# A hybrid encoder step: input projection, gated linear attention and convolution merged into one program on one core

## The chip, the cores and the metric

One Trainium2 chip, one core of it. The metric is the device time of one execution in microseconds (us). The engines are called TensorE (PE in the rows; its weight loads PEld), VectorE (DVE), ScalarE (ACT), GpSimd (POOL) and SyncE (SP, which only issues DMAs here). Each runs its own instructions in order and waits on semaphores.

## The reference

One layer over 2048 tokens of a new stream and 64 tokens of a running one, width 1024, all in float32:

```python
x = layer_norm(x, ln_in_g, ln_in_b)
gq, gk, gv, gr, glow, sq, sk, sv, cb, cc, ch = split_cols(x @ w_in)   # 3088 columns
lg = log_sigmoid(glow @ w_gate_up + b_gate) / 16
# gated linear attention, 4 heads, blocks of 64 tokens with a state S
b = cumsum(lg); att = einsum('bhtk,bhsk,bhtsk->bhts', q, k, exp(b_t - b_s))   # causal
o = (q * exp(b)) @ S + att @ v
S = exp(b_last) * S + (k * exp(b_last - b))^T @ v
go = o * rsqrt(mean(o*o) + eps) * gla_norm_g * silu(gr)
# stick-breaking attention so over sq, sk, sv;  convolution
co = cb * causal_conv3(cc * ch)
mix = concat(go, so, co) @ w_out
x = LN(alpha * x + mix);  x = LN(alpha * x + relu(x @ w_up)^2 @ w_down)
```

The outputs are both x, the new keys and values sk and sv, the attention states and the last two rows of cc * ch of each stream.

## The kernel before

Three programs follow each other, with a barrier of all engines between them: `phase_in`, `phase_gla`, `phase_tail`. They hand data on through scratch memory in HBM (`zt_scratch`, features by tokens; `gv_scratch`, tokens by features; `mixt_scratch`; `xn_scratch`).

**phase_in** normalises x in tiles of 128 tokens (ScalarE's square root, three VectorE instructions, one addition on POOL), stores the normalised rows, transposes them on TensorE (`ps_t`, L357) and splits them into a high and a low part (`xh`, `xl`, double-buffered by token group). The token groups are 512, 512, 512 and 576 tokens long. Weights come in six chunks of 512 or 528 columns, each loaded again for each token group, copied by ScalarE (L272, `wh`) and reduced by VectorE to a low part (L329, `wl`). A product is three float32r matmuls for each of eight slices of the contraction (`split_product`, L111 to L113): xh by wh, xh by wl, xl by wh. "F" units have features in rows and up to 512 tokens as columns; "T" units (gv, keys and values) have 128 tokens in rows and 512 features as columns. Six PSUM banks hold results, ScalarE evacuates them (L279) and issues their stores.

**phase_gla** works in groups of 512 tokens (and the 64 of the running stream), and within a group in tiles of 128 tokens. Work "ahead" for a group: the gate (TensorE, ScalarE), the running sum of it (`gate_sum`, VectorE scans), `decay`, and six levels: for each, VectorE forms differences of sums (`level_arg`, L744, L745), ScalarE takes exp (L661), VectorE multiplies with k and q (`level_mul`, L754, L760), TensorE forms products (`level_product`, L859) and VectorE writes the valid part into `att` (`level_put`, L790); the diagonal follows (L866). Work for a tile, here called a body: k's transpose (`turn`), `kv` (L891), `intra` (L903), `inter` (L924), the new state (L809), the squares' sums (L934), root, and gating (L820, L823). The list `order` interleaves a group's bodies with the next group's ahead. POOL works through the convolution on its own: ten pieces of 512 (or 64) tokens, for each three loads, a product and six instructions, a store, all issued on POOL's queue (L948 to L983).

**phase_tail** does the stick-breaking attention, the output projection and the feed-forward block. It has its own loads of constants (L1360) and is not touched.

The lines that follow are the functions that the diff touches.

Of the kernel before, what the change touches and what calls it, by code (L numbers as in the profile page):

```python
# [114 lines left out]


# [3 lines left out]
def phase_in(nc, x_tile, ln_g, ln_b, w_in, ident_in, xn_dram, zt_dram, token_stores, lasting):  # L120
    WW = 528
    chunks = [
        ([(C_GQ, 512)], "F", Z_GQ),
        ([(C_GR, 528)], "F", Z_GR),
        ([(C_GV, 512)], "T", "gv"),
        ([(C_SQ, 256), (C_CB, 256)], "F", Z_SQ),
        ([(C_SK, 512)], "T", "kv"),
        ([(C_CC, 512)], "F", Z_CC),
    ]
    NCH = len(chunks)  # L130
    WSTAGE, OUTS, BANKS = 4, 4, 6
    s = Scope(nc, "p1")
    with s:
        ident = s.sb("ident", [P, P])
        g_b = s.sb("g_b", [P, D])
        b_b = s.sb("b_b", [P, D])
        xs = s.sb("xs", [P, 2, D])
        xn = s.sb("xn", [P, 2, D])
        stats = s.sb("stats", [P, 2, 12])
        mv = s.sb("mv", [P, 2, 2])  # L140
        rstd = s.sb("rstd", [P, 2, 1])
        eps = s.sb("eps", [P, 1])
        xh = s.sb("xh", [P, 2, KT, NMAX], F32R)
        xl = s.sb("xl", [P, 2, KT, NMAX], F32R)
        wst = s.sb("wst", [P, WSTAGE, WW])
        wh = s.sb("wh", [P, 2, KT, WW], F32R)
        wl = s.sb("wl", [P, 2, KT, WW], F32R)
        outb = s.sb("outb", [P, OUTS, 512])
        ps_t = s.ps("ps_t", [P, 2, 512])
        ps_m = s.ps("ps_m", [P, BANKS, 512])  # L150

        ident_loaded, rows_in = s.sem("ident_loaded"), s.sem("rows_in")
        eps_set = s.sem("eps_set")
        x_in = s.sems("x_in", 2)
        stats_done = s.sem("stats_done")
        var_done = s.sem("var_done")
        std_done = s.sem("std_done")
        rstd_done = s.sem("rstd_done")
        centred = s.sem("centred")
        scaled = s.sem("scaled")  # L160
        normed = s.sem("normed")
        xn_out = s.sems("xn_out", 2)
        turned = s.sem("turned")
        xhi_done = s.sem("xhi_done")
        xlo_done = s.sem("xlo_done")
        w_inn = s.sems("w_in", WSTAGE)
        whi_done = s.sem("whi_done")
        wlo_done = s.sem("wlo_done")
        unit_done = s.sem("unit_done")
        evacuated = s.sem("evacuated")  # L170
        out_st = lasting.results


        gtiles, n = [], 0
        for (t0, cnt) in GROUPS:
            gtiles.append([(n + i, o, c) for i, (o, c) in enumerate(subtiles(t0, cnt, P))])
            n += len(gtiles[-1])

        units = []
        for g, (t0, cnt) in enumerate(GROUPS):  # L180
            for c, (pieces, kind, where) in enumerate(chunks):
                gc = g * NCH + c
                width = sum(w for _, w in pieces)
                if kind == "F":
                    for m0 in range(0, width, P):
                        mw = min(P, width - m0)
                        for o, cc in moving(cnt):
                            units.append(dict(g=g, gc=gc, kind="F", m0=m0, mw=mw, o=o, n=cc, t0=t0, row=where + m0))
                else:
                    for o, cc in subtiles(t0, cnt, P):  # L190
                        units.append(dict(g=g, gc=gc, kind="T", o=o, n=cc, t0=t0, what=where))
        by_chunk = {}
        for i, u in enumerate(units):
            by_chunk.setdefault(u["gc"], []).append((i, u))
        chunk_end = {gc: us[-1][0] + 1 for gc, us in by_chunk.items()}

        order = [("norm", 0, gtiles[0][0]), ("weights", 0)]
        for i, t in enumerate(gtiles[0]):
            order += [("norm", 0, x) for x in gtiles[0][i + 1:i + 2]] + [("turn", 0, t)]
        for g in range(len(GROUPS)):  # L200
            for c in range(NCH):
                gc = g * NCH + c
                if gc + 1 < NCH * len(GROUPS):
                    order.append(("weights", gc + 1))
                ahead = [(g + 1, t) for t in gtiles[g + 1][c:c + 1]] if g + 1 < len(GROUPS) else []
                order += [("norm", *x) for x in ahead] + [("product", gc)] + [("turn", *x) for x in ahead]

        block = s.stack.enter_context(nc.Block())

        @block.sync  # L210
        def _(sp):
            for what, *a in order:
                if what == "norm":
                    j, o, c = a[1]
                    if j >= 2:
                        sp.wait_ge(centred, j - 1)
                    sp.dma_start(xs[:c, j % 2, :], x_tile(j)).then_inc(x_in[j % 2], 16)
                    if j == 0:
                        load_row_broadcast(sp, g_b[:], ln_g, rows_in)
                        load_row_broadcast(sp, b_b[:], ln_b, rows_in)  # L220
                        sp.dma_start(ident[:], ident_in).then_inc(ident_loaded, 16)
                elif what == "weights":
                    gc = a[0]
                    for k in range(KT):
                        u = gc * KT + k
                        if u >= WSTAGE:
                            sp.wait_ge(wlo_done, u - WSTAGE + 1)
                        slot, at = u % WSTAGE, 0
                        pieces = chunks[gc % NCH][0]
                        for c0, w in pieces:  # L230
                            sp.dma_start(wst[:, slot, at:at + w], w_in[k * P:(k + 1) * P, c0:c0 + w]).then_inc(w_inn[slot], 16)
                            at += w


        def n_stores(i):
            return sum(1 if units[j]["kind"] == "F" or units[j]["what"] == "gv" else 2 for j in range(i % OUTS, i + 1, OUTS))


        slot_loads = [0] * WSTAGE
        loads_by_unit = []  # L240
        for u in range(NCH * len(GROUPS) * KT):
            slot_loads[u % WSTAGE] += len(chunks[(u // KT) % NCH][0])
            loads_by_unit.append(slot_loads[u % WSTAGE])

        @block.scalar
        def _(act):
            for what, *a in order:
                if what == "norm":
                    g, (j, o, c) = a
                    act.wait_ge(eps_set, 1)  # L250
                    act.wait_ge(var_done, j + 1)
                    if j >= 2:
                        act.wait_ge(centred, j - 1)
                    act.activation(rstd[:c, j % 2, :], mv[:c, j % 2, 1:2], ACT.Sqrt, bias=eps[:c, :]).then_inc(std_done, 1)
                elif what == "turn":
                    g, (j, o, c) = a
                    for q in range(2):
                        act.wait_ge(turned, 2 * j + q + 1)
                        if g >= 2 and q == 0:
                            act.wait_ge(unit_done, chunk_end[(g - 1) * NCH - 1])  # L260
                        act.activation(xh[:, g % 2, 4 * q:4 * q + 4, o:o + c],
                                       ps_t[:, q, :].rearrange("p (k t) -> p k t", k=4)[:, :, :c],
                                       ACT.Copy).then_inc(xhi_done, 1)
                elif what == "weights":
                    gc = a[0]
                    width = sum(w for _, w in chunks[gc % NCH][0])
                    for k in range(KT):
                        u = gc * KT + k
                        act.wait_ge(w_inn[u % WSTAGE], 16 * loads_by_unit[u])
                        if gc >= 2 and k == 0:  # L270
                            act.wait_ge(unit_done, chunk_end[gc - 2])
                        act.activation(wh[:, gc % 2, k, :width], wst[:, u % WSTAGE, :width], ACT.Copy).then_inc(whi_done, 1)  # L272
                else:
                    for i, u in by_chunk[a[0]]:
                        act.wait_ge(unit_done, i + 1)
                        if i >= OUTS:
                            act.wait_ge(out_st[i % OUTS], 16 * n_stores(i - OUTS))
# [15 lines left out]
        def _(dve):  # L293
            dve.memset(eps[:], LN_EPS).then_inc(eps_set, 1)
            for what, *a in order:
                if what == "norm":
# [6 lines left out]
                    if j >= 2:  # L303
                        dve.wait_ge(std_done, j - 1)
# [42 lines left out]
        def _(pe):  # L347
            pe.wait_ge(ident_loaded, 16)
            for what, *a in order:
# [9 lines left out]
                elif what == "product":  # L359
# [5 lines left out]
                    for i, u in by_chunk[gc]:  # L365
# [12 lines left out]
                        mm.then_inc(unit_done, 1)  # L378

# [1536 lines left out]
```

## Time and profile before

| | |
|---|---|
| median of 3 runs | 3112.1 us (3108.27 to 3112.32) |
| profiled execution | 3112.7 us, its span 3110.9 us |
| mean granted TensorE clock | 0.934 |
| TensorE busy | 2734.4 us (88%) |
| VectorE busy | 1505.1 us (48%) |
| ScalarE busy | 1069.5 us (34%) |
| POOL busy | 329.9 us (11%) |

Busy time is the union of an engine's instructions, matmuls overlap in it. Shares are means over stages that are bound in different ways, so the rows below are cut by stage.

### The profile page before, as it was taken

The numbers are of one execution on the slowest core, as the hardware profiler recorded it, in microseconds if no ns is written. First come the engines' busy times: TensorE is split into PE (matmuls) and PEld (weight loads), VectorE is DVE, ScalarE is ACT, GpSimd is POOL, SyncE is SP. The second block draws the span as 40 slices with busy tenths as digits, with TensorE's granted clock in tenths as the row PEclk, the third lists the DMA queues.
The fourth block names the chain that finished last, engine by engine and source line by source line (L and its number), as shares of the span: only waits on it lengthen the run. The fifth ranks groups of instructions, "written<-read, shape, count | busy, mean of one in ns | idle before, by whom it ended". The sixth has DMA issues, their size and how long they took to land. (4 is left out here: it accounts for less than half of the span.)

```text
span 3110.9 us, 38667 instructions
## 1 busy us (share of the span) xinstructions
PE 2734.4 (88%) x13838; PEld 2268.3 (73%) x13838; DVE 1505.1 (48%) x2247; ACT 1069.5 (34%) x1783; POOL 329.9 (11%) x283
## 2 busy tenths in 40 slices
PE   5999999946662467999998999999999988999997
PEld 4787789835541356888877888877888766888885
DVE  5333342158883556665656544446644425522224
ACT  3323333223342424443443444443434321322221
POOL 1100010056600000000001100001100000000000
PEclk9999999966786588999999999999999989999998
DMA  5544454233315654575655766565766554544452
GB/s 185 169 160 153 160 180 126 85 121 88 89 45 187 191 191 140 169 249 179 216 193 191 229 218 209 191 206 183 234 190 227 170 171 144 190 157 158 154 168 98
DMA packets 362107, 526.11 MB, mean 169 GB/s; under 512 B 28832, under 2 KB 208208, under 8 KB 361920
## 3 DMA queue, kind: packets, MB, share of 16 engines
q1 hardware_dynamic: 337696, 480.23, 48.1%
q10 hardware_dynamic: 18832, 26.10, 2.3%
q0 software_dynamic: 5392, 17.31, 1.6%
q8 instruction: 115, 1.88, 0.3%
q14 instruction: 72, 0.59, 0.1%
HBM read 422.74 MB, written 100.80 MB: 168 GB/s over the span
## 5 line engine op out<-in xcount | busy, mean ns | idle before, releaser
L111 PE MATMUL p_ps_u<-p_xh,p_wh 128*128 128x512 f32 (+1 forms) x1280 | 453.1, 354 | 5.4 <-DVE p_xl L1626 5.4
L112 PE MATMUL p_ps_u<-p_xh,p_wl 128*128 128x512 f32 (+1 forms) x1280 | 451.5, 353 | 0.0
L113 PE MATMUL p_ps_u<-p_xl,p_wh 128*128 128x512 f32 (+1 forms) x1280 | 451.0, 352 | 0.0
L1575 DVE SCALAR_TENSOR_TENSOR p_res<-p_res,p_ps_d 128x512 f32<-128x512 f32 (+1 forms) x340 | 232.1, 685 | 451.4 <-PE p_ps_d L113 445.7
L111 PE MATMUL p_ps_d<-p_wh,p_hh 128*128 128x512 f32 (+1 forms) x1088 | 433.2, 398 | 16.9 <-DVE p_res L1575 14.8
L112 PE MATMUL p_ps_d<-p_wh,p_hl 128*128 128x512 f32 (+1 forms) x1088 | 428.6, 394 | 0.0
L113 PE MATMUL p_ps_d<-p_wl,p_hh 128*128 128x512 f32 (+1 forms) x1088 | 428.4, 394 | 0.0
L1484 ACT ACTIVATE p_wh<-p_wst 128x1024 fp32r<-128x1024 f32 x288 | 293.9, 1049 | 276.6 <-PE p_ps_d L113 225.0
L1633 DVE TENSOR_TENSOR p_r<-p_r 128x512 f32<-128x512 f32 (+1 forms) x160 | 95.8, 599 | 461.3 <-ACT p_hh L1514 461.3
L1507 ACT ACTIVATE p_r<-p_ps_u 128x512 f32<-128x512 f32 (+1 forms) x160 | 83.8, 524 | 579.5 <-PE p_ps_u L113 579.4
L111 PEld LDWEIGHTS p_ps_u<-p_xh,p_wh 128*128 128x128 f32 x1280 | 241.2, 188 | 35.5 <-DVE p_xl L1626 6.2
L113 PEld LDWEIGHTS p_ps_u<-p_xl,p_wh 128*128 128x128 f32 x1280 | 241.2, 188 | 31.0
L112 PEld LDWEIGHTS p_ps_u<-p_xh,p_wl 128*128 128x128 f32 x1280 | 241.2, 188 | 28.3
L111 PEld LDWEIGHTS p_ps_d<-p_wh,p_hh 128*128 128x128 f32 (+1 forms) x1088 | 204.0, 187 | 66.4 <-DVE p_res L1575 19.1
L111 PE MATMUL p_ps_m<-p_xh,p_wh 128*128 128x512 f32 (+3 forms) x680 | 242.4, 356 | 1.4 <-DVE p_xl L320 1.4
L112 PE MATMUL p_ps_m<-p_xh,p_wl 128*128 128x512 f32 (+3 forms) x680 | 242.9, 357 | 0.0
L113 PE MATMUL p_ps_m<-p_xl,p_wh 128*128 128x512 f32 (+3 forms) x680 | 241.2, 355 | 0.0
L113 PEld LDWEIGHTS p_ps_d<-p_wl,p_hh 128*128 128x128 f32 (+1 forms) x1088 | 203.4, 187 | 48.3
L329 DVE TENSOR_TENSOR p_wl<-p_wst,p_wh 128x512 fp32r<-128x512 f32 (+1 forms) x192 | 127.6, 703 | 224.6 <-ACT p_wh L272 224.4
L112 PEld LDWEIGHTS p_ps_d<-p_wh,p_hl 128*128 128x128 f32 (+1 forms) x1088 | 204.1, 188 | 44.0
L1715 POOL TENSOR_TENSOR p_aw<-p_sg,p_keep 128x512 f32<-128x512 f32 (+2 forms) x84 | 89.9, 1070 | 1363.3 <-DVE p_keep L1671 1363.3
L1544 ACT ACTIVATE p_tg<-p_ps_z 128x512 f32<-128x512 f32 (+5 forms) x168 | 87.4, 520 | 323.1 <-PE p_ps_z L1796 322.9
(155 smaller groups left out, 4473.0 us busy)
## 6 DMA issues: line engine op xcount, KB each, us to landing
p_wl<-wlo_scratch SPq DMA_DIRECT2D x216, 512.0 KB, 5.1
p_wst<-in_w_up SPq DMA_DIRECT2D x128, 512.0 KB, 6.0
p_wst<-in_w_down SPq DMA_DIRECT2D x128, 512.0 KB, 4.6
wlo_scratch<-p_wl SPq DMA_DIRECT2D x72, 512.0 KB, 3.6
p_wst<-in_w_in SPq DMA_DIRECT2D x128, 256.0 KB, 3.6
p_kk<-ks_scratch SPq DMA_DIRECT2D x84, 256.0 KB, 5.9
p_vv<-vs_scratch SPq DMA_DIRECT2D x84, 256.0 KB, 4.5
p_wst<-in_w_out SPq DMA_DIRECT2D x32, 512.0 KB, 6.0
```

Source lines behind the costliest of these rows:

```text
L111: pe.matmul(out, lhs_hi, rhs_hi, start=first, stop=False, skip_group_check=skip)
L112: pe.matmul(out, lhs_lo, rhs_hi, start=False, stop=False, skip_group_check=skip)
L113: return pe.matmul(out, lhs_hi, rhs_lo, start=False, stop=last, skip_group_check=skip)
L329: dve.tensor_tensor(wl[:, gc % 2, k, :width], wst[:, u % WSTAGE, :width], wh[:, gc % 2, k, :width].bitcast(F32), ALU.subtract).then_inc(wl ...
L1484: act.activation(wh[:, u % WRING, :], wst[:, u % WSTG, :], ACT.Copy).then_inc(whi_done, 1)
L1507: act.activation(r[:, i % 2, :cc], ps_u[:, i % 2, :cc], ACT.Relu).then_inc(relu_done, 1)
L1544: act.activation(tg[:m, n % SIG, 512 - w:512], ps_z[:m, :w], ACT.Sigmoid, scale=-SCALE).then_inc(sig_done, 1)
L1575: dve.scalar_tensor_tensor(out=acc, in0=acc, scalar=scale, in1=ps_d[:c, d % DB, :], op0=ALU.mult, op1=ALU.add).then_inc(d_free, 1)
L1633: dve.tensor_tensor(r[:, i % 2, :cc], r[:, i % 2, :cc], r[:, i % 2, :cc], ALU.mult).then_inc(sq_done, 1)
L1715: pool.tensor_tensor(aw[:m, u % AW, i, :w], sg[:m, n % SIG, :w], keep[:m, n % KEEP, 513 - w:513], ALU.mult).then_inc(a_pool, 1)
```

## The change

`phase_in` and `phase_gla` become one program, `phase_head`. One hand-written list `order` is run by all five engines.

- Groups of attention have 256 tokens (nine: eight of 256, one of 64). The gate's two products share one bank, the level products of both heads share one, a tile's four heads share one bank and one gating instruction.
- The projection's F units keep their columns (512, or 2 x 288 in the last group), the 16 gate columns are a unit of their own with weights kept in SBUF. T units have 256 columns in place of 512. Weights are loaded in units of 512 KB into a staging ring of two (`wst`), split into a ring of four (`wh`, `wl`). Three PSUM banks (`DB`) are shared by products and the transposes of x. `xh` and `xl` have one buffer; the next group's tiles are transposed between the T products of the last pair.
- The normalisation is done in place, with two fused VectorE instructions, and rstd is a power on POOL. The first group's T products begin with its first tile.
- A slot of attention follows each F product and every second T product. It holds one step of the current group's bodies and one step of a later group's ahead. An ahead starts two products after the last gr unit of its token group. What is left when the products end follows without products between.
- The convolution has 18 pieces of 256 (or 64) tokens. POOL computes, SyncE issues loads and stores.

```diff
+def phase_head(nc, a, x_tile, xn_dram, zt_dram, gv_dram, mixt_dram, k_p, v_p, k_s, v_s, lasting):
+    WRING, WSTG, DB, OUTS, XS = 4, 2, 3, 4, 5
+    GN = 256
+    GG = [(t, GN) for t in range(0, SEQ, GN)] + [(SEQ, DEC)]
...
+        def ahead_slots(g):
+            slots = [[("load", g)]] if g % 2 == 0 else []
+            slots += [[("gate", g), ("gate_log", g)], [("gate_sum", g)], [("decay", g), ("level_arg", g, 0), ("silu_exp", g)],
+                      [("level_mul", g, 0), ("level_arg", g, 1)]]
+            for li in range(NL):
+                slot = [("level_product", g, li)]
+                if li + 1 < NL:
+                    slot.append(("level_mul", g, li + 1))
+                if li + 2 < NL:
+                    slot.append(("level_arg", g, li + 2))
+                slot.append(("level_put", g, li))
...
+        def tile_slots(g):
+            js = group_tiles[g]
+            slots = [[("v_in", j) for j in js] + [("k_turn", js[0])], [("kv", js[0])]]
+            for j in js:
+                cs, more = tiles[j][3], [j + 1] if j + 1 in js else []
+                slots.append([("intra", j), ("inter", cs[0]), ("state", cs[0])] + [("k_turn", x) for x in more])
+                if len(cs) > 1:
+                    slots.append([("inter", cs[1]), ("state", cs[1]), ("squares", j)])
+                else:
+                    slots[-1].append(("squares", j))
+                slots.append([("sums", j), ("root", j)] + [("kv", x) for x in more])
+                slots.append([("gated", j)])
+            return slots
...
+        for i, step in enumerate(dense):
...
+            order.append(step)
...
+            if step[0] in ("F", "T"):
+                split_weights(i)
+                dense_at[step[:3] if step[0] == "F" else step[:4]] = len(dense_at)
+                if step[0] == "F" or step[3] % 2 == 1:
+                    take_slot()
+                ready = [dense_at.get(("F", min(t // 512, 3), conv_f), len(dense_at)) for x, t, cnt in conv]
+                if conv_put < len(conv) and ready[conv_put] + 2 <= len(dense_at):
+                    order += [("c_load", conv_put), ("conv", conv_put)]
+                    conv_put += 1
...
+        @block.sync
...
+                elif what == "w_load":
+                    u = at[0]
+                    if u >= WSTG:
+                        sp.wait_ge(wlo_done, u - WSTG + 1)
...
+                elif what == "c_load":
+                    k = at[0]
+                    x, t, cnt = conv[k]
+                    if x == 0:
+                        wait_stores(sp, results_of(min(t // 512, 3), conv_f))
+                    if k:
+                        sp.wait_ge(c_out, 16 * k)
+                    for n, z in enumerate((Z_CC, Z_CH, Z_CB)):
+                        sp.dma_start(cin[:, n, :cnt], zt_dram[z + P * x:z + P * x + P, t:t + cnt]).then_inc(c_in, 16)
...
+                elif what == "conv":
+                    k = at[0]
+                    x, t, cnt = conv[k]
+                    sp.wait_ge(c_y, 6 * (k + 1))
+                    sp.dma_start(mixt_dram[768 + P * x:768 + P * x + P, t:t + cnt], cin[:, 1, :cnt]).then_inc(c_out, 16)
...
+        @block.scalar
...
+                elif what == "w":
+                    u = at[0]
+                    act.wait_ge(w_loaded[u % WSTG], 16 * (u // WSTG + 1))
+                    if u >= WRING:
+                        act.wait_ge(m_mm, unit_count[u - WRING])
+                    act.activation(wh[:, u % WRING, :], wst[:, u % WSTG, :], ACT.Copy).then_inc(whi_done, 1)
...
-        phase_in(nc, x_tile, a["ln_in_g"], a["ln_in_b"], a["w_in"][0], a["ident"], xn_dram, zt_dram, token_stores, lasting)
-        phase_gla(nc, a, zt_dram, gv_dram, mixt_dram, lasting)
+        phase_head(nc, a, x_tile, xn_dram, zt_dram, gv_dram, mixt_dram, k_p, v_p, k_s, v_s, lasting)
```

In the order that this gives, the projection has 136 products, and 100 of them are followed by a place for a slot. Convolution pieces 0 to 3, 4 to 7 and 8 to 11 stand behind F products 16 and 17 and the first two T products of a group's third pair; pieces 12 to 17 stand in the last group behind F products 16 and 17 and the first four T products. `v_in` of tile 12, `kv` of tile 12, all of bodies 6 to 8 and of ahead 7 and 8 stand behind the last product.

## Rows read from the trace of the kernel before

**Rows 1.** The page's first line.
```profile
span 3110.9 us, 38667 instructions
```

**Rows 2.** Stages: us, busy of each engine (instructions), granted clock, DMA share, GB/s.
```profile
42.00:638.00 596.00, 595.28 (x2960) 493.12 (x2960) 183.18 (x289) 186.60 (x342) 38.45 (x26) 1.00 0.45 146
638.00:655.00 17.00, 2.46 (x3) 0.92 (x4) 3.97 (x4) 1.99 (x3) 7.79 (x5) 0.63 0.70 222
655.00:958.00 303.00, 178.85 (x1162) 141.62 (x1161) 243.64 (x400) 113.41 (x147) 129.59 (x121) 0.74 0.28 78
sum 958.00, PE 784.44 PEld 641.94 DVE 457.33 ACT 314.50 POOL 188.10; mean PE 196.11 PEld 160.49 DVE 114.33 ACT 78.63 POOL 47.03
```

**Rows 3.** Timeline of TensorE: start us, us, instruction, idle before; two stretches.
```profile
38.91 1.97 PE L357 MATMUL p_ps_t<-p_ident,p_xn 128*128 128x128 f32 x8 [3.34 <-POOL p_xn L339]
42.29 0.79 PE L111 MATMUL p_ps_m<-p_xh,p_wh 128*128 128x512 f32 x1 [1.41 <-DVE p_xl L320]
...
1903.09 0.28 PE L1822 MATMUL p_ps_o<-p_atl,p_vv 128*128 128x256 f32 x1
1903.21 0.40 PE L111 MATMUL p_ps_u<-p_xh,p_wh 128*128 128x512 f32 x1
1903.44 0.39 PE L112 MATMUL p_ps_u<-p_xh,p_wl 128*128 128x512 f32 x1
```

**Rows 4.** Timeline of TensorE in attention, at full clock.
```profile
817.78 1.95 PE L859 MATMUL p_ps_l<-p_qb,p_ex 128*128 128x128 f32 x16
...
824.68 0.68 PE L891 MATMUL p_ps_s<-p_v,p_kt 64*64 64x128 f32 x16
```

**Rows 5.** Timeline of VectorE in attention, POOL idle.
```profile
893.48 0.60 DVE L809 SCALAR_TENSOR_TENSOR p_st<-p_st,p_eb,p_ps_s 128x128 f32<-128x128 f32 x2
...
894.60 1.40 DVE L760 TENSOR_TENSOR p_qb<-p_ex,p_gq 64x512 f32<-64x512 f32 x2
896.02 1.30 DVE L790 COPY_PREDICATED p_att<-p_masks,p_ps_l 128x512 f32<-128x512 int32 x2
...
923.34 0.46 DVE L760 TENSOR_TENSOR p_qb<-p_ex,p_gq 64x64 f32<-64x64 f32 x2
```

**Rows 6.** Groups by line: busy us, mean ns, idle before and releaser.
```profile
L1484 ACT ACTIVATE p_wh<-p_wst 128x1024 fp32r<-128x1024 f32 x288 | 293.9, 1049 | 276.6 <-PE p_ps_d L113 225.0 <-DMA p_wst<-in_w_up 20.5 <-DMA p_wst<-in_w_out 15.7
...
L1602 DVE TENSOR_TENSOR p_wl<-p_wst,p_wh 128x1024 fp32r<-128x1024 f32 x72 | 86.1, 1219 | 28.3 <-ACT p_wh L1484 28.3
...
L279 ACT ACTIVATE p_outb<-p_ps_m 128x512 f32<-128x512 f32 (+4 forms) x119 | 64.4, 541 | 281.0 <-PE p_ps_m L113 272.4 <-ACT p_outb L279 7.3 <-issue 1.2
```

**Rows 7.** Timeline of POOL: convolution pieces from first instruction to store.
```profile
655.76 0.10 POOL L957 MEMSET p_cu<- 128x2 f32 x1 [6.81 <-DMA p_cb<-zt_scratch]
...
669.14 0.61 POOL L979 DMA_DIRECT2D mixt_scratch<-p_cy  x1 [0.30 <-POOL p_cy L974]
...
713.75 0.19 POOL L959 COPY p_cu<-p_cu 128x2 f32<-128x2 f32 x1 [3.82 <-DMA p_cb<-zt_scratch]
...
724.48 0.60 POOL L979 DMA_DIRECT2D mixt_scratch<-p_cy  x1 [0.30 <-POOL p_cy L974]
...
845.68 0.31 POOL L962 TENSOR_TENSOR p_cu<-p_cc,p_ch 128x64 f32<-128x64 f32 x1 [5.32 <-DMA p_cu<-in_state_conv]
...
849.12 0.60 POOL L979 DMA_DIRECT2D mixt_scratch<-p_cy  x1 [0.29 <-POOL p_cy L974]
```

**Rows 8.** DMA issues by line: queue, count, KB each, median us to landing.
```profile
p_wst<-in_w_up SPq DMA_DIRECT2D x128, 512.0 KB, 6.0
p_wst<-in_w_in SPq DMA_DIRECT2D x64, 128.0 KB, 2.5
mixt_scratch<-p_cy POOLq DMA_DIRECT2D x8, 256.0 KB, 2.4
```

**Rows 9.** Timeline of all engines: attention's last VectorE instruction, the tail's first load.
```profile
955.23 0.43 DVE L823 TENSOR_TENSOR p_on<-p_on,p_gg 128x256 f32<-128x256 f32 x1
...
959.72 0.35 SPq L1360 DMA_DIRECT2D p_ident<-in_ident  x1
```

More of the change, by code:

```diff
@@ L179, in phase_in @@
[L179 to L232, printed above, removed]
@@ new lines, in phase_head, with weights, t_steps @@
+        gla_f = [i for i, f in enumerate(fs) if f[2] == Z_GR + 384][0]
+        conv_f = [i for i, f in enumerate(fs) if f[2] == Z_CB + 128][0]
+        pairs = [C_GV, C_GV + 256, C_SK, C_SV]
+        wunits, dense, f_unit = [], [], {}
+        def weights(*what):
+            wunits.append(what)
+            return len(wunits) - 1
+        def t_steps(g, p):
+            u = weights("T", pairs[p], 0)
+            weights("T", pairs[p], 1)
+            return [("T", g, p, ti, u) for ti in range(len(gtiles[g]))]
@@ new lines, in phase_head, with take_slot @@
+        aheads, bodies = [ahead_slots(g) for g in range(NG)], [tile_slots(g) for g in range(NG)]
+        ag = body = 0
+        dense_at, order, next_w, drained = {}, [], 0, False
+        conv, conv_put = [(x, t, cnt) for t, cnt in GG for x in range(2)], 0
+        def take_slot():
+            nonlocal ag, body
+            found, a_before = [], ag
+            if body < NG and ag > body:
+                found += bodies[body].pop(0)
+                if not bodies[body]:
+                    body += 1
+            if a_before < NG and a_before <= body + 1:
+                f = dense_at.get(("F", source(a_before), gla_f))
+                if f is not None and (drained or f + 2 <= len(dense_at)):
+                    found += aheads[a_before].pop(0)
+                    if not aheads[a_before]:
+                        ag += 1
+            order.extend(found)
+            return bool(found)
@@ L792, in _ @@
+                    last.then_inc(lev_put, 1)
+                elif what == "state":
                     c = at[0]
@@ L908, in _ @@
                         pe.wait_ge(intra_done, 1)
-                elif step == "inter":
+                elif what == "inter":
                     c = at[0]
@@ L930, in _ @@
                     pe.wait_ge(sq_done, j + 1)
-                    pe.wait_ge(gate_y, gates_seen)
+                    if gates_seen[("sums", j)]:
+                        pe.wait_ge(gate_y, 2 * gates_seen[("sums", j)])
                     if j:
                         pe.wait_ge(n_ln, j)
-                    pe.matmul(ps_g[:, :4 * m], ones[:, :], sq[:, :4 * m], start=True, stop=True).then_inc(n_mm, 1)
-                    tiles_seen = j + 1
-        pieces = [(x, t, n) for x in range(2) for t, n in GG]
```

1088 lines of the change are left out of this document (531 added, 557 removed).

## Prediction

> **What bounds the kernel now.** I read the stages first. From 42 to 638 us, the input projection, TensorE is busy 595 of 596 us at full clock, while VectorE works 183 and ScalarE 187 [rows 2]. From 655 to 958 us, linear attention, VectorE is busiest with 244 of 303, TensorE has 179 at a mean granted clock of 0.74, and nobody is full. Between them lie 17 us in which hardly anything runs. So one stage is TensorE alone, the next a chain of short pieces led by VectorE. The tail starts at 959.7, 4 us after the last VectorE instruction of attention [rows 9]; the change doesn't touch it. All that can be won lies before 959.7, of a span of 3110.9 us [rows 1].
>
> **What would be perfect.** The products stay, and attention's instructions are laid between them. VectorE's 457 us before 958 and ScalarE's 315 (the sums [rows 2]) are both below TensorE's share, so if nobody waited TensorE would set the end. I price the pieces, then what waits.
>
> **Products.** 593 us: 596, less 3 for the first dozen matmuls, at the 1.2 GHz level (0.79 us long against 0.40 later [rows 3]); and the 4 tiles transposed before them, 4 x 1.0. The T products (tokens in rows) become 256 columns wide: 4 x 17 x 24 = 1632 matmuls instead of 816 of 512. In the tail a 256-column matmul, weight load included, starts 0.12 us before the next, a 512-column one 0.23 [rows 3]: 1632 x 0.118 - 816 x 0.231 = +4. Total 601.
> If the load were not hidden, T would cost more. The Trainium skill, "TensorE: Matmul & The Clock Gate", section "LDWEIGHTS (loading the stationary operand)", puts a load at columns/1.2 ns, some 107 ns for 128; added instead of hidden that would be 175 us by that page. The trace speaks for hiding: 0.12 is the whole step.
>
> **Attention on TensorE.** At full clock 16 fp32 instructions of 128 columns take 1.95 us, 0.122 each, kv's 16 small ones 0.68 [rows 4]. Per 256 tokens: 64 level instructions, 7.8; the gate, as 8 of them, 1.0; intra and inter 32, 3.9; kv 1.4; sums (as 16) and turns (4), 2.4: 16.5.
>
> **Start.** Before, the last of four tiles' transposes start at 38.9 and the first product at 42.3, so a tile takes 3.4 us from the one to the other [rows 3]. The new code starts T products with tile 0, but TensorE waits for all ten constants, VectorE for the narrow gate weights, and weights 2 and 3 (each a 6.0 us load [rows 8] into a staging slot that must first be split) stand ahead of tile 1's statistics on VectorE. I put the first product at 30 (20 to 36). Each tile's transposes now stand directly ahead of its own two products, so TensorE sees that time: 4 x 5.7 of products + 3 x 3.3 + 2.5 of low clock = 35. The first F product comes at 65 with 8 T products (22.7) done; before had done 20 by then. Worth 3 us, no more.
>
> **Up to the mark.** I call the end of the sixteenth F product of the last token group the mark: there SyncE meets the first of the last six convolution pieces. 601 less the 27 done at 65 us, less 34 behind the mark (one F, ten T), is 540. By the order, the slots before it hold ahead 0 to 5 and the start of 6, bodies 0 to 4 and most of 5: 98 us. Sum 638. Waits in it:
> - *SyncE held by convolution, 32 us.* The convolution's loads and stores move from POOL's queue to SyncE's, so SyncE waits in line for POOL. A 512-column piece takes 10.7 us from first instruction to store, the first one 13.4, a 64-column one 3.4 [rows 7]. For 256 that gives 6.5 and, at the first piece's rate, 8.1; I take 6.8. Around it: 0.5 to issue the store, 2.1 until it has landed (2.4 for twice the bytes), 1.4 for three loads' issue, 2.5 for landing [rows 8]: 13.3 per piece. Four stand behind four neighbouring products, and the weight loads behind them can't be issued. SyncE is through after 2.5 + 10.7 + 3 x 13.3 and a group's load, 56 us. The weights of the next group's second T pair need 6.0 + 1.05 + 1.2 more [rows 6, 8], 64.3. TensorE wants them after one F, twelve T, four turns and their slots: 51 to 54. That is 11 for each of three groups. Bounds: pieces of 11.5 give about 4 each, pieces of 16 about 22.
> - *Turns in the shared banks, 8 us.* Two tiles are transposed back to back in three banks that the products use too: about 2.5 at three group ends.
> - *Round trip between ScalarE and VectorE, 12 us.* In a level slot: evacuation 0.6 and its store's issue, as a load's 0.35 [rows 9], weight copy 1.05, VectorE's split 1.2, state 0.6, three multiplies 1.3 (two are 1.40 at 512, 0.46 at 64) and two differences 0.7 at the same rate, ScalarE's exp of 512 columns at the copy's rate 0.6 [rows 5, 6]: 6.4, with hand-overs 7 to 7.5. TensorE's step is 5.5 + 1.0 + about 0.9 = 7.4. They are level; the 13 norms that fall in, some 4 us each, push VectorE behind in part of the 30 such steps. 0 to 60.
> - *Semaphore steps, 5 us.*
> The mark is at 65 + 638 + 57 = 760.
>
> **Behind the mark.** TensorE would be through its products 45 us later. But SyncE has six pieces in line before v_in of tile 12: 53 for four, 3 for another store and a group's load, and two of 64 columns with a wait for their state, about 13 each: 82. v_in lands 3.5 later, at 86, and kv of tile 12 and everything behind it in each queue waits some 40 us. Then, without cover, group 7's levels: multiplies 1.3, differences 0.7, puts 0.75 (1.30 the pair at 512), state or gating 0.6 or 1.4 [rows 5]: 3.5 x 6 = 21, with decay and the last two levels 31; group 8's 64 tokens, latency-bound, 24; body 8 alone 10. 65 in all (55 to 80).
> The last VectorE instruction comes at 760 + 86 + 65 = 911 instead of 955.7, 45 us earlier [rows 9]. The span becomes 3066, with the 1.8 us around it (this execution: 3112.7) 3068; the median of the runs shown is 0.6 below this execution: **3067 us**.
>
> POOL's norm addition (17 tiles) goes to VectorE inside fused instructions; VectorE's time for a tile stays about the same, and is hidden as now.
>
> **A rule against the change.** The first convolution piece took 13.4 us beside a working VectorE, a later one 10.7 [rows 7]; now all 18 run beside VectorE. At that 25% each piece costs 14.6, and the sum is 4 x 1.3 for each of the three groups and about 7 behind the mark, 22 us, longer. The Trainium skill, "SBUF — State Buffer", section "SBUF: two separate sides", states an exclusive lock between GpSimd and a VectorE operation with two SBUF inputs, the loser fully blocked. The trace agrees in direction; its 25% is the size here.
>
> **Rivals.**
> 1. *SyncE's waits are largely covered* (0.20). Pieces at their lower bound, 11.5, take off 3 x 7 and 12 behind the mark, a drain at its floor of 55 another 10: 3024. For it: TensorE has up to three weight units in hand. Against: v_in stands behind all six pieces in any case.
> 2. *The round trip becomes the bound, and the kernel is slower* (0.10). ScalarE copies weights only after evacuating, VectorE splits only after the copy, and exp waits for VectorE ahead of the next evacuation. Place: the 30 level steps over F products. It decides when a step exceeds TensorE's 7.4 us by more than (45 + 12)/30 = 1.9 on average; at 3.0, VectorE stretched by POOL and norms, 33 us past that: 3145. For it: a late evacuation holds one of three banks. Against: the durations add to 7.5.
> 3. *Part of the gain goes in both places* (0.15): pieces of 15, three groups +20, behind the mark +9: 3096.
> 4. *No change that can be measured* (0.05): the same with a drain of 80, 3112.
>
> **Numbers.** My forecast has 0.50 and a range of its own, 3040 to 3090. With rivals 1 and 3, 3008 to 3122 leaves out most of rival 2 and a little below. Faster by over 0.2% (6 us, about what a measurement of this kernel can tell): 0.50 + 0.20 + 0.15, less 0.02 for the top of rival 3, where it meets the bound: 0.83. Same 0.06, slower 0.11.
>
> **What the profile after would show.** The tail's first load at 915. T matmuls 0.118 apart. TensorE full from 65 us to the mark but for a gap near 10 us, ended by a load or split of weights, at each group's second T pair; a gap of about 40 us before kv of tile 12, ended by v_in; SyncE waiting for POOL. I am wrong if kv of tile 12 comes at once, or if TensorE idles before most level products for VectorE, or in products for ScalarE's evacuation (rival 2).

## The result: 0.7% slower, and the profile after

The changed kernel takes 3134.3 us (median of 4 runs, 3131.7 to 3136.2), the kernel before 3111.9 beside it: ratio 1.0074, 95% interval 1.0056 to 1.0091. The forecast was 3067 us. The result lies outside its range, and on the other side of no change.

The first line of the page and, from the DMA issues by line, the weight loads of the projection (answers to [rows 1] and [rows 8]):

```profile
span 3131.8 us, 40707 instructions
...
p_wst<-in_w_in SPq DMA_DIRECT2D x96, 512.0 KB, 3.9
```

Windows of the changed kernel: from about the first F product to the mark, from there to the last product, from there to the tail's first load at 977.0. Columns as in [rows 2].

```profile
72.00:798.00 726.00, 673.94 (x4164) 587.38 (x4164) 357.90 (x611) 261.99 (x404) 87.91 (x110) 0.95 0.46 143
798.00:838.00 40.00, 40.00 (x328) 39.08 (x326) 20.56 (x42) 10.15 (x20) 18.98 (x24) 1.00 0.31 92
838.00:977.00 139.00, 55.73 (x280) 41.36 (x280) 47.59 (x139) 25.89 (x53) 11.56 (x21) 0.61 0.18 37
```

The plan works for the most part: from 72 to 838 us TensorE is busy 714 of 766 us. But the last of these windows shows 139 us in which TensorE works 56 and VectorE, which [rows 2] had as the leader of attention, only 48. And the granted clock of the first window is 0.95, where the projection of the kernel before had 1.00 [rows 2]. The tail begins at 977.0 instead of 959.7 [rows 9].

TensorE's timeline behind the last product (start, duration, instruction, idle before it and what ended it):

```profile
839.00 0.44 PE L920 MATMUL p_ps_k<-p_ident,p_ksf 128*128 128x128 f32 x2
848.50 2.07 PE L889 MATMUL p_ps_g<-p_glow,p_wgu 16*128 16x256 f32 x4 [9.07 <-DMA p_gk<-zt_scratch]
899.48 2.30 PE L936 MATMUL p_ps_s<-p_v,p_kt 64*64 64x128 f32 x16 [48.90 <-DMA p_v<-gv_scratch]
```

And SyncE's queue in the same time:

```profile
800.33 1.33 SPq L492 DMA_DIRECT2D p_cin<-zt_scratch  x3
811.44 0.32 SPq L501 DMA_DIRECT2D mixt_scratch<-p_cin  x1
813.13 1.30 SPq L492 DMA_DIRECT2D p_cin<-zt_scratch  x3
...
838.19 7.30 SPq L492 DMA_DIRECT2D p_cin<-zt_scratch  x3
858.04 0.32 SPq L501 DMA_DIRECT2D mixt_scratch<-p_cin  x1
858.40 0.44 SPq L505 DMA_DIRECT2D out_conv_state_p<-p_cu  x1
859.78 1.27 SPq L492 DMA_DIRECT2D p_cin<-zt_scratch  x3
...
888.77 0.43 SPq L505 DMA_DIRECT2D out_conv_state_s<-p_cu  x1
889.25 0.93 SPq L477 DMA_DIRECT2D p_v<-gv_scratch  x2
```

Six convolution pieces stand ahead of the load of v for tile 12. Each holds the queue from its three loads to its store (800.3 to 811.4 for the first). The load is issued at 889.25, and kv of tile 12 starts at 899.48. The wait of 48.9 us is the one that the prediction called 40, in the place that it named.

What SyncE waited for before its convolution stores, over the whole kernel (total us, times, longest), from the waits of its queue:

```profile
SPq L501 <- POOL p_cin L829: 187.1, 18, 12.5
```

That is 10.4 us before each of the 18 stores.

The same hold inside the products, from the timeline of all engines at the end of the first token group:

```profile
205.27 0.32 SPq L501 DMA_DIRECT2D mixt_scratch<-p_cin  x1
205.63 0.43 SPq L449 DMA_DIRECT2D p_wst<-in_w_in  x1
...
209.53 1.06 ACT L537 ACTIVATE p_wh<-p_wst 128x1024 fp32r<-128x1024 f32 x1 [8.27 <-DMA p_wst<-in_w_in]
210.49 0.37 ACT L546 ACTIVATE p_outb<-p_ps_m 128x256 f32<-128x256 f32 x1
...
210.95 0.55 PE L111 MATMUL p_ps_m<-p_wh,p_xh 128*128 128x256 f32 x1 [7.00 <-issue]
```

A weight load is issued right behind a convolution store. ScalarE has stood 8.3 us for it, and behind that copy in ScalarE's order stands the evacuation of a bank that TensorE's next product needs. So TensorE stops 7.0 us for weights that it doesn't want yet (they are those of the next group's first T pair): in an in-order queue the waiting instruction takes along what stands behind it.

The granted clock at the start, windows of 5 us of the changed kernel (columns as above):

```profile
40.00:45.00 5.00, 3.08 (x26) 2.84 (x26) 1.87 (x3) 1.47 (x3) 0.00 (x0) 1.00 0.15 52
45.00:50.00 5.00, 5.00 (x31) 5.00 (x31) 3.46 (x6) 0.39 (x1) 0.55 (x1) 0.66 0.27 108
50.00:55.00 5.00, 3.08 (x26) 2.84 (x25) 1.56 (x3) 1.47 (x3) 0.00 (x0) 1.00 0.15 52
55.00:60.00 5.00, 5.00 (x31) 5.00 (x31) 2.20 (x2) 0.38 (x1) 0.00 (x0) 0.66 0.26 105
```

From 42.6 TensorE stands still 1.9 us for VectorE's split of the transposes. Then it runs on, and the window from 45 to 50, which has no gap, has a mean clock of 0.66: part of these 5 us is at 1.2 GHz (0.5), the rest at 2.4. This repeats for each of three tiles. By the trace's clock records there are 14 such stretches before 800 us, of 3.4 to 10.2 us each, 78 us together. Thirteen lie beside an idle gap of TensorE of over 1 us, the other one (at 629.3) behind two gaps of 0.5 us.

### The profile page after: what moved, and what is told of

Same layout as the page of the kernel before. It is cut to its first block and busy times, and to the rows that moved or that the text cites. A ratio compares the mean times of both kernels' runs of the same rounds, so it can differ in the third digit from the quotient of the medians.

```text
span 3131.8 us, 40707 instructions
## 1 busy us (share of the span) xinstructions
PE 2756.6 (88%) x14670; PEld 2328.9 (74%) x14670; DVE 1501.9 (48%) x2346; ACT 1065.7 (34%) x1768; POOL 266.5 (9%) x285
## 5 line engine op out<-in xcount | busy, mean ns | idle before, releaser
L676 DVE TENSOR_TENSOR p_wl<-p_wst,p_wh 128x1024 fp32r<-128x1024 f32 x96 | 118.0, 1236 | 356.1 <-ACT p_wh L537 355.8
L111 PE MATMUL p_ps_m<-p_xh,p_wh 128*128 128x512 f32 (+1 forms) x640 | 234.0, 366 | 0.0
L112 PE MATMUL p_ps_m<-p_xh,p_wl 128*128 128x512 f32 (+1 forms) x640 | 228.6, 357 | 0.0
L113 PE MATMUL p_ps_m<-p_xl,p_wh 128*128 128x512 f32 (+1 forms) x640 | 228.4, 357 | 0.0
L111 PE MATMUL p_ps_m<-p_wh,p_xh 128*128 128x256 f32 (+1 forms) x544 | 165.1, 303 | 41.4 <-DVE p_xl L671 18.8
```

The source lines that it names most:

```text
L111: pe.matmul(out, lhs_hi, rhs_hi, start=first, stop=False, skip_group_check=skip)
L112: pe.matmul(out, lhs_lo, rhs_hi, start=False, stop=False, skip_group_check=skip)
L113: return pe.matmul(out, lhs_hi, rhs_lo, start=False, stop=last, skip_group_check=skip)
L676: dve.tensor_tensor(wl[:, u % WRING, :], wst[:, u % WSTG, :], wh[:, u % WRING, :].bitcast(F32), ALU.subtract).then_inc(wlo_done, 1)
```

## The experiments

Each ratio is against the kernel before, run beside it on the same chip. Its medians there were 3112.4 (for e1, e2, e3), 3112.1 (e4 to e7) and 3113.2 (e8, e9, e10), so the times can be set beside the changed kernel's 3134.3 too.

**v_in of tiles 12 and 13 ahead of the last six pieces** (e1_v_first).

```diff
+        for j, k in ((12, 12), (13, 14)):
+            order.remove(("v_in", j))
+            order.insert(order.index(("c_load", k)), ("v_in", j))
```

> Only two DMA issues move in SyncE's order: v_in of tiles 12 and 13 stand ahead of the last six convolution pieces instead of behind them. Theory A (my main one: the convolution that holds SyncE makes v_in late, and everything behind kv of tile 12 waits for it): in the profile of the changed kernel TensorE stands still for 48.9 us before kv of tile 12 and starts it at 899.5; with v_in there, kv follows the gate product at about 851, and the whole drain moves with it by up to 48 us, less what is late next (v_in of tiles 14 and 15 and the gated store of tile 11 still stand behind the six pieces, until about 889): 3086 to 3100. Rival B (the drain is set by group 7's levels in ScalarE and VectorE, not by kv): group 7's gate was free at 848 already, its level chain could have begun there but stands behind kv in TensorE's order only; then the gain is what that chain is not slowed by, under 15 us: 3120 to 3134.

Measured: 3100.9 us (3095.8 to 3104.2), ratio 0.9964 (0.9951 to 0.9977). TensorE's timeline there:

```profile
854.74 2.07 PE L892 MATMUL p_ps_g<-p_glow,p_wgu 16*128 16x256 f32 x4 [12.36 <-DMA p_gk<-zt_scratch]
856.74 2.31 PE L939 MATMUL p_ps_s<-p_v,p_kt 64*64 64x128 f32 x16
```

kv follows the gate at once, 42.7 us sooner. The time falls 33 us and not 43. Most of the difference is the next v_in, of tiles 14 and 15, late in turn: it still stood behind the pieces, was issued at 897.2, and kv of tile 14 waited 8.0 us. Theory A holds, 0.9 us beyond the slow end of its range. Two moved DMA issues turn the loss into a small gain.

**The convolution's DMAs back on POOL's queue** (e2_conv_pool).

```diff
         @block.sync
-                elif what == "c_load":
-                    ...
-                elif what == "conv":
-                    ...
         @block.gpsimd
+                elif what == "c_load":
+                    ...
+                    for n, z in enumerate((Z_CC, Z_CH, Z_CB)):
+                        pool.dma_start(cin[:, n, :cnt], zt_dram[...]).then_inc(c_in, 16)
                 elif what == "conv":
                     ...
+                    pool.wait_ge(c_y, 6 * (k + 1))
+                    pool.dma_start(mixt_dram[...], cin[:, 1, :cnt]).then_inc(c_out, 16)
```

> The convolution's loads and stores are issued from POOL's queue again, as in the kernel before; everything else as in the changed kernel. Theory A (SyncE held by the convolution): the four gaps at group ends that stand before the third pair of the last T products of a group (7.0, 3.8, 5.7 us) and the two before a later T pair (1.8, 3.9) go, 22 us with their low clock behind them worth another 15; the 9.1 before gate 7 and most of the 48.9 before kv of tile 12 go too, since SyncE is free at the mark: 3134 - 37 - 50 = about 3047, 3035 to 3070. Rival C (the weights, not the convolution, hold SyncE, since it waits 374 us for VectorE's splits before the next weight loads): the group-end gaps stay, and the time falls by the 50 us of the drain at most: 3080 to 3090. Rival D (what is issued from POOL's queue costs the same somewhere else, by slower pieces or a late rstd for the norms): 3110 or more.

Measured: 3044.7 us (3042.8 to 3048.2), ratio 0.9788 (0.9773 to 0.9803). TensorE behind the last product:

```profile
805.54 0.44 PE L917 MATMUL p_ps_k<-p_ident,p_ksf 128*128 128x128 f32 x2
805.91 1.12 PE L886 MATMUL p_ps_g<-p_glow,p_wgu 16*128 16x256 f32 x4
806.97 1.38 PE L933 MATMUL p_ps_s<-p_v,p_kt 64*64 64x128 f32 x16
```

No wait before the gate, none before kv. The five gaps at the group ends are gone, and the last product ends at 804.5 instead of 838.0. Theory A holds (it said about 3047), C and D fall. This one queue is worth 89.6 us, more than the whole difference between forecast and result.

**The convolution on SyncE, but a piece's store one slot behind its loads** (e10_store_later).

```diff
+        def conv_turn(ready_now):
+            if unstored:
+                order.append(("c_store", unstored.pop()))
+            elif ready_now:
+                order.extend([("c_load", conv_put), ("conv", conv_put)])
+                unstored.append(conv_put)
+                ...
```

> The changed kernel with the convolution still on SyncE, but a piece's store is put one slot behind its loads, and the next piece's loads one slot behind that, so SyncE seldom waits for POOL. Theory A (SyncE's waiting for POOL is what costs): most of what POOL's own queue brought comes back, the gaps at group ends go, and the 48.9 us before kv of tile 12 shrink to under 15: 3050 to 3075. If it is the issue of these transfers on SyncE, not the wait, that costs (54 loads and 18 stores, 0.5 us each): 3095 or more.

Measured: 3058.8 us (3054.8 to 3062.4), ratio 0.9821 (0.9806 to 0.9836). 75 of the 90 us come back with all 72 transfers still issued by SyncE, and the five gaps at the group ends are gone. So it was for the most part the waiting in line, not the issuing. Two late loads of v are left, as in this row; the other is 7.4 us before kv of tile 14:

```profile
819.54 2.31 PE L946 MATMUL p_ps_s<-p_v,p_kt 64*64 64x128 f32 x16 [10.64 <-DMA p_v<-gv_scratch]
```

Whether the 14 us between this run and e2_conv_pool are such waiting or the issuing was not tried.

**Extra work in TensorE's gaps** (e3_fill, then e4_fill_short). The filler's products are read by nobody.

```diff
+                if FILL.get((what, *at)):
+                    ...
+                    for _ in range(FILL[(what, *at)]):
+                        pe.matmul(ps_k[:, 256:384], glh[:]..., gll[:]..., start=True, stop=True, ...)
```

> Nothing but extra work on TensorE, 733 matmuls of 128x128 on constants into unused columns of a bank, whose result nobody reads. They stand directly in front of the 18 instructions before which TensorE stood still for over 1 us up to the last products (51 us of gaps in all), each filler about 0.3 us shorter than its gap. Theory E (each gap costs more than its length, since the granted clock is 1.2 GHz for 3.4 to 10.2 us within the same stretch: 14 such episodes, 78 us together, before 800 us, where the kernel before had none in its projection): with the gaps filled the clock stays at 2.4 GHz, and the last products end up to 39 us earlier; the time falls to 3100 to 3120, since the drain behind it does not shorten. Rival F (the low clock costs nothing of its own, because TensorE is behind other engines there anyway): no change, 3134, or slower by the fillers that meet no gap, up to 3145.

Measured: 3155.1 us (3151.1 to 3157.4), ratio 1.0139 (1.0121 to 1.0157). The table holds 702 matmuls, not 733. They were far longer than meant, as this row shows:

```profile
200.58 11.70 PE L848 MATMUL p_ps_k<-p_gll,p_glh 128*128 128x128 f32 x103
```

That is 11.7/103 = 0.114 us each, and the gap there had been 7.0. The time lies above both ranges, and since the fillers were longer than their gaps, the run decides nothing between the two theories. The second try was sized by that row (394 matmuls, not 398):

> The changed kernel with fillers on TensorE again, now sized by what one took in the run with 733 of them: 0.114 us for a matmul of 128x128, so that 398 of them span 46 of the 51 us of gaps. In the two places where TensorE had still stood for 4.6 and 7.1 us before the filler (it waited for ScalarE's copy of the turned keys), the filler now writes another bank that is free there. Theory E (a gap costs the low clock behind it as well): no episode at 1.2 GHz between 42 and 800 us, the last products end 25 to 39 us before the 838.0 of the changed kernel, and the time is 3095 to 3112. Rival F (the low clock behind a gap costs nothing): the last products end at 838 or later, 3134 to 3140.

Measured: 3130.5 us (3129.6 to 3133.2), ratio 1.0058 (1.0043 to 1.0073). Neither theory's range. At the start it is clean. The two windows that had 0.66 now read:

```profile
45.00:50.00 5.00, 5.00 (x44) 5.00 (x43) 2.81 (x5) 0.60 (x2) 0.55 (x1) 1.00 0.36 134
...
55.00:60.00 5.00, 5.00 (x45) 5.00 (x44) 0.07 (x1) 1.38 (x4) 0.00 (x0) 1.00 0.36 140
```

The first F product comes at 67.2 instead of 72.4, with TensorE held up as long as before at each tile. The three stretches at 1.2 GHz were 10.2 us together, half of that is 5.1, and 5.2 came back. Behind the start it is not clean. Windows from the first F to the last product, of the changed kernel and then of this run:

```profile
72.40:838.00 765.60, 713.54 (x4487) 626.06 (x4484) 378.46 (x653) 272.13 (x423) 106.89 (x134) 0.96 0.45 140
```

```profile
67.20:834.20 767.00, 744.08 (x4839) 659.89 (x4836) 377.06 (x653) 272.14 (x423) 107.61 (x134) 0.98 0.45 140
```

Less the fillers' 43.3 us, TensorE's own work fell from 713.5 to 700.8, 12.8 us. But fillers and idle time together grew from 52.1 to 66.2, 14.2 us. My reading: what TensorE waits for there is released by other engines and loads, which the fillers don't make sooner, so a TensorE that works faster meets it earlier and waits longer. Of seven gaps of 1.0 to 2.7 us that are left before 800 us, five stand right behind a filler, which fits. But a filler that outlasts its gap costs time too, and this run can't tell the two apart. So a cost of the low clock apart from the wait is shown only at the start, where the thing waited for moves with TensorE.

**The next tile's transposes between a tile's two T products** (e7_pool_start; on e2_conv_pool).

```diff
-                    dense += [("turn", 0, ti)]
-                    ...
-                    dense += [one[ti], two[ti]]
+                    dense += [one[ti]]
+                    if ti < 3:
+                        dense += ... + [("turn", 0, ti + 1)] + ...
+                    dense += [two[ti]]
```

> The kernel with the convolution on POOL's queue (3044.7); the transposes of the next tile stand between a tile's two T products at the start instead of ahead of the first, so that their evacuation and split lie beside the second. Three gaps of 1.9 us stood there, each with 3.4 us at 1.2 GHz behind it. If the gap and the clock behind it both cost: 3 x 1.9 + 3 x 1.7 = 11 off, first F product at 61 instead of 72.4, 3034. If the clock costs nothing: 6 off, 3039. If a tile's statistics are late instead (its normalisation would stand before the transposes that come 3 us earlier): nothing, 3044.

Measured: 3034.5 us (3033.1 to 3037.3), ratio 0.9752 (0.9735 to 0.9768): 10.2 off e2_conv_pool. The window from 40 us to the first F product, which now comes at 60.6, is full and at full clock:

```profile
40.00:60.60 20.60, 20.60 (x176) 20.58 (x175) 9.86 (x14) 4.48 (x10) 0.55 (x1) 1.00 0.25 91
```

11.8 us earlier: 5.8 of it are the three gaps, and half of the 10.2 us at 1.2 GHz is 5.1, as the first of the three theories had it.

**Earlier loads** (e6_pool_early; on e2_conv_pool). The load of gate, queries and keys for an even group needs only the first five F products. It goes three products earlier, and v_in of tiles 2 to 11 one earlier.

```diff
+        for g in range(0, NG, 2):
+            order.insert(order.index(("load", g)), ("load_r", g))
+            if g < 8:
+                sooner(("load", g), 3)
+        ...
+        for j in range(2, 12):
+            sooner(("v_in", j), 1)
...
-                    wait_stores(sp, results_of(source(g), gla_f))
+                    wait_stores(sp, results_of(source(g), 4))
```

> The kernel with the convolution on POOL's queue (3044.7), with the loads of an even group's gate, queries and keys three products earlier (they need only the first five F products; the load for the silu stays) and v_in one product earlier. Theory H (the gaps before gate 0, kv 2, gate 2, kv 6, kv 10, together 12.5 us, are SyncE issuing these loads one product ahead, behind weight loads that wait for VectorE): those gaps go and the low clock behind them with it, 12 + about 12 x 0.7: 3022 to 3036. Rival: the chain of the gate is late anyway (the gap of 4.7 before the first level product stays), and the whole brings under 6 us: 3039 to 3045.

Measured: 3020.6 us (3019.8 to 3022.0), ratio 0.9704 (0.9690 to 0.9719). Windows from first F to last product of e2_conv_pool, then of this run:

```profile
72.40:804.50 732.10, 703.21 (x4487) 615.62 (x4484) 384.30 (x653) 272.63 (x423) 145.89 (x194) 0.98 0.47 149
```

```profile
69.80:775.80 706.00, 690.95 (x4487) 607.52 (x4485) 383.66 (x653) 272.53 (x423) 144.56 (x195) 1.00 0.49 155
```

The same 4487 matmuls; idle time falls from 28.9 to 15.1 us and TensorE's own work from 703.2 to 691.0, because its clock goes from 0.98 to 1.00. Here the cause of the gaps was taken away and not their length filled, and both parts are kept: 26 us in this stretch for 12.5 us of gaps named beforehand. The whole, 24.1 us under e2_conv_pool, is 1.4 us more than the fast end of the range. Theory H holds; one of the gaps that are left is the rival's, 4.7 us before the first level product, and it didn't hold the gain up.

**An attention slot after every T product** (e5_pool_dense; on e2_conv_pool), and the same **in the last group's last two T pairs only** (e9_dense_end; on e8).

```diff
-                if step[0] == "F" or step[3] % 2 == 1:
+                if step[0] == "F" or step[3] % 2 == 1 or True:
                     take_slot()
...
+                if step[0] == "F" or step[3] % 2 == 1 or (step[1] == 3 and step[2] >= 2):
```

> The kernel with the convolution on POOL's queue (3044.7), plus an attention slot after every T product instead of every second one: 18 more slots stand beside products, and fewer behind them (there the rest took 88 us after the last product). Theory G (a slot behind the products costs about 2.4 us, beside them only TensorE's 1 to 2 us of work, since VectorE is busy 52 to 60% there): 18 x 2.4 = 43 off the drain, 18 x about 1.0 more waiting before: 3015 to 3030. Rival B again (the round trip of ScalarE and VectorE in a level slot, some 7 us, doesn't fit a T product of 2.8 us): TensorE stands still 4 us in each, with the low clock behind it, and it gives all of it back: 3044 to 3065.

Measured: 3105.8 us (3102.3 to 3110.4), ratio 0.9982 (0.9973 to 0.9991): 61 us slower than e2_conv_pool. Its window from first F to last product, and a row of TensorE's timeline in it:

```profile
72.40:886.90 814.50, 733.07 (x4535) 641.54 (x4535) 398.49 (x673) 283.44 (x438) 148.87 (x199) 0.95 0.44 135
```

```profile
617.74 1.65 PE L900 MATMUL p_ps_l<-p_qb,p_ex 128*128 128x128 f32 x6 [4.29 <-DVE p_att L734]
```

Idle time rises from 28.9 to 81.4 us, the clock falls to 0.95, and the last product ends 82 us later. What stands behind it shrinks by 20 us only (from 87.0 to 67.1). The loss goes far beyond the range of rival B too, and the 18 slots were a miscount: by the two kernels' order, attention steps stand at 118 places between products instead of 87, 31 more, for 82 us more before the last product. And there was little to win: only 48 more attention matmuls stand beside products (4535 against 4487), a few slots' work. The last 512 tokens' attention can't begin before their own products, so slots taken earlier run empty later.

**The three repairs together** (e8_pool_early_start), and with the five late slots (e9_dense_end).

> The three repairs together: convolution on POOL's queue (68 us under the kernel before), loads of the gate and v_in earlier (24 more), the next tile's transposes between a tile's two T products at the start (10 more). They act in different stretches (start, group boundaries, behind the products), so if each gap costs on its own the gains add: 3044.7 - 24 - 10 = 3011, 3007 to 3015. If an earlier start only lets TensorE run into the next late load, part is lost: 3015 to 3021.

Measured: 3006.8 us (3005.7 to 3009.0), ratio 0.9655 (0.9642 to 0.9668): the gains add. The two measured apart, 24.1 and 10.2, would give 3010.4.

> The same, plus an attention slot after every T product in the last token group's third and fourth T pair alone: five more slots stand beside products. No weights are left to split there, so VectorE and ScalarE are freer than in the other places where a slot after each T product cost 82 us. Theory G there: 5 slots x 2.4 us off the drain, 5 x 1 to 2 us more TensorE before: 3001 to 3008. Rival B (the 7 us round trip of a level slot, not VectorE's load, is what doesn't fit a T product): each extra slot lets TensorE wait 2 to 4 us, as much as it saves: 3008 to 3016.

Measured: 3002.5 us (2997.7 to 3006.9), ratio 0.9640 (0.9625 to 0.9655), 4.4 us under e8, whose runs its own just overlap. The last product ends 14.0 us later (778.6 against 764.6), the tail begins 4.8 us earlier (847.4 against 852.2). By its order, attention steps stand at 94 places between products instead of 89, and the same steps are left behind the last product as in e5_pool_dense: the same 48 matmuls moved, for 14 us instead of 82. This version beats both kernels: 3.6% under the one before, 4.2% under the changed one.

## Why the prediction was wrong

The forecast's span was 3066 and the profiled one is 3131.8. The 65.8 us between them (65.7 by the rounded rows), along the prediction's own steps:

| Step | Predicted | Measured | Off by |
|---|---|---|---|
| first F product | 65 | 72.4 | +7.4 |
| first F to last product | 740 (to 805) | 765.6 (to 838.0) | +25.6 |
| last product to kv of tile 12 | 41 (846) | 61.5 (899.5) | +20.5 |
| kv of tile 12 to the tail | 69 (915) | 77.6 (977.0) | +8.6 |
| the tail | 2151.2 | 2154.8 | +3.6 |

**The start.** The first product comes at 33.2 us, where I had 30. The transposes take 1 us less than I had. The rest of the 7.4 us is the three stretches of low clock, 5.1, beside the 2.5 that I had priced.

**Up to the mark: the step that failed first.** It read "601 ... dense" and "98" of attention at full clock, and added the waits as bare idle time. The waits were sized well in sum: 57 predicted, 52.1 measured to the last product. Their places weren't; see below. The work itself came to 691 us at a mean clock of 1.00 (e6_pool_early), where I had 638 + 45 = 683, 8 too little. What was missing is the clock: 713.5 - 691.0 = 22.5 us, and 5.1 of the first row's 7.4. With the waits 5 less than I had, 22.5 + 8 - 5 is the row's 25.6. I priced every matmul at full clock; the change brought gaps into that stage, and I carried its old clock over. Of those 28 us only the 5 at the start are shown to be a cost apart from the waits (e4_fill_short, e7_pool_start). The rest goes only together with what causes the gaps.

The Trainium skill, "TensorE: Matmul & The Clock Gate", in its table "Terms", puts the penalty at the throttled time times one minus the clock's share, half of it here. At the start the runs agree (10.2 us low, 5.2 back). Over the stretch from the first F to the last product that would be 34 us of the 68.3 low there, and the runs show 22.5. TensorE was idle in 15 of these 68 us, so the rule goes too far by that; half of the 53 busy ones would be 27.

**The waits inside it.** *SyncE held by convolution, 32 us*: right in cause. e2_conv_pool takes 33.5 us out of this stretch, but as 23.2 of idle time and 10.3 of TensorE's own work, while my 32 were idle time alone: that the sums agree is luck. The prediction's piece cycle of 13.3 us was 11.7 to 14.5 at the three group ends and 12.8 and 11.8 in the queue shown above. The 14.6 of the rule against the change was neared by two pieces only. The place was wrong too: most of it (7.0, 3.8 and 5.7 us) stands ahead of the third product of a group's last T pair, six T products before the one that I named, since ScalarE's queue passes SyncE's hold on to an evacuation. In the named place stand 1.8 and 3.9 us. *Semaphore steps, 5 us* should have been late loads: the gate, kv and first level products of even groups waited for loads issued one product ahead, 26 us with their clock (e6_pool_early). *The round trip of ScalarE and VectorE, 12 us* and *shared banks, 8 us* were too dear; with those loads early, 15.1 us of idle time is left for everything.

**Behind the mark: the second step that failed.** The mechanism was right (e1_v_first, e2_conv_pool), the size short. SyncE was through with the pieces at 889, 91 us after the mark (about 798), not 82: the last three, those of the prompt's end and of the 64 tokens, took 21.6, 14.8 and 14.6 us from loads to loads where I had about 13. kv of tile 12 started 10.2 us after the issue of its v_in, for which I had taken 3.5. With the last product 40 us behind the mark instead of 45, these make the 20.5. Why that took 10.2 was not tried.

**The drain** of 65 us, called 55 to 80, took 73.3 to VectorE's last instruction (972.8), within that range; e2_conv_pool has 84.5 from kv of tile 12 to the tail.

**The tail** is the same code. It took 2.3 to 6.7 us longer in the changed kernel and all ten variants than in the kernel before. In the changed kernel its first 260 us have 3.8 us more at 1.2 GHz (171.1 against 167.3, by the clock records). No run was made to find the cause.

**The rivals.** Rival 2, the round trip as the bound, was the only one on the right side, at nearly the measured time (3145), and it isn't what happened: gaps of over 1 us before level products are 8.5 of the 52 us. e5_pool_dense shows where a round trip does decide, with a slot on each T product. Of the signs that I named for being wrong one came true in part: TensorE did idle within products for ScalarE's evacuation, but because ScalarE stood for a weight load, not for VectorE. All others stayed away. Of what I said one would see, the T matmuls' step (0.12), the wait before kv of tile 12 and SyncE's waiting for POOL were there; the gap near 10 us at each group's second T pair and the tail's first load at 915 were not. So the forecast had most of its causes and erred in prices and places, the prices nearly all in one direction: it let every wait cost its own length, once. What made the kernel slower than before is the queue: with the convolution's DMAs left on POOL's, the same change makes it 68 us faster (e2_conv_pool).

## What to carry to other kernels

When a change fuses a full stage with a gappy one, price it at both clocks: here 14 stretches of 3.4 to 10.2 us at 1.2 GHz stood beside TensorE's gaps. Then ask of every wait that is put on an in-order queue who stands behind it in that queue, and who stands behind those in theirs: 18 stores that each wait 10 us for POOL on SyncE cost 75 to 90 us of 3134, through weight loads, a bank's evacuation and a late v. And before filling gaps, move what ends them: fillers in all 18 gaps gave back 4 us, loads issued one to three products earlier, for 12.5 us of gaps, gave 24.

## What the runs showed of the hardware

At full clock an fp32r matmul of 128x128 on 128 columns, with its weight load, starts every 0.114 us (103 of them in 11.70), one of 256 columns every 0.12 and one of 512 every 0.23 [rows 3]. So 128 columns take hardly less time than 256. The Trainium skill, "TensorE: Matmul & The Clock Gate", section "LDWEIGHTS (loading the stationary operand)", gives 107 ns for a load of 128 columns; 0.114 is near that, but no run here separates the load from the product.
